# The recurrent block in token products: four convolution tiles computed block by block, the other tiles, states and gate alternating, ScalarE's functions grouped

## The reference

```
def rglru_block(x, w_in, conv_w, conv_b, w_rgate, b_rgate, w_igate, b_igate, lam, w_o):
    gate, u = jnp.split(x @ w_in, 2, axis=-1)
    u = causal_depthwise_conv(u, conv_w, conv_b)          # four taps
    ub = u.reshape(bsz, s, LRU_BLOCKS, LRU_BLOCK_W)
    r = sigmoid(einsum('bshi,hij->bshj', ub, w_rgate) + b_rgate)
    i = sigmoid(einsum('bshi,hij->bshj', ub, w_igate) + b_igate)
    log_a = -LRU_C * r * softplus(-lam)
    a = exp(log_a)
    b_in = sqrt(-expm1(2.0 * log_a)) * (i * u)
    h[t] = a[t] * h[t-1] + b_in[t]                        # the scan
    y = h * gelu(gate)
    return y @ w_o
```

## Time and profile before

| | |
|---|---|
| Median of 3 runs | 2240.7 us (2238.72 to 2241.26) |
| Profiled execution | 2240.25 us |
| Its span in the trace | 2239.0 us |
| Mean granted TensorE clock | 0.974 |
| TensorE busy | 2085.5 us |
| VectorE busy | 1544.3 us |
| ScalarE busy | 1179.8 us |

### The profile page before, as it was taken

The page is one execution under the profiler, slowest core; times in us unless marked ns, Lnnn a source line. Parts: engine busy times, 40 slices in busy tenths (PEclk is TensorE's granted clock), DMA queues, the critical chain, the costliest instruction groups (busy, mean ns, idle before and its releaser), DMA issues.

```text
span 2239.0 us, 33115 instructions
## 1 busy us (share of the span) xinstructions
PE 2085.5 (93%) x13325; PEld 1876.8 (84%) x13325; DVE 1544.3 (69%) x2678; ACT 1179.8 (53%) x2047; POOL 73.5 (3%) x126
## 2 busy tenths in 40 slices
PE   7999999898999989999998998998987999999998
PEld 7778899787799978889987777997976999877997
DVE  4685777787677686576777767777466766666766
ACT  4454555494455555445545536554454555565554
POOL 3000000010000010000000000001000000000000
PEclk9999999999999999999999999999998999999999
DMA  8424566455366654456543436664524666424663
GB/s 262 151 76 142 181 186 186 134 162 183 119 188 181 185 152 129 135 166 192 181 155 130 145 127 190 187 191 133 157 72 148 187 193 183 160 85 148 183 193 107
DMA packets 412008, 356.17 MB, mean 159 GB/s; under 512 B 16242, under 2 KB 353398, under 8 KB 411856
## 3 DMA queue, kind: packets, MB, share of 16 engines
q1 hardware_dynamic: 405104, 332.49, 49.0%
q0 software_dynamic: 6752, 21.57, 2.9%
HBM read 352.97 MB, written 1.05 MB: 158 GB/s over the span
## 4 chain that ended last, share of the span: by engine, by line
PE 79%; DVE 14%; ACT 4%; DMA 2%; issue 1%; POOL 1%; SPq 0%; DVEq 0%; ACTq 0%
PE psum L720 18%; PE psum L722 18%; PE psum L721 18%; PE psum L1230 15%; DVE w_lo L1820 4%; PE psum L1125 3%; PE psum L1111 1%; DVE small L2176 1%; DVE n_tok L2173 1%; PE psum L814 1%; PE psum L895 1%; PE psum L1054 1%; DMA tok<-in_mem_dram 1%; DVE qt L2247 1%; DVE x_tok L2195 1%
## 5 line engine op out<-in xcount | busy, mean ns | idle before, releaser
L1820 DVE TENSOR_TENSOR w_lo<-w_raw,w_hi 128x1024 fp32r<-128x1024 f32 x639 | 749.5, 1220 | 150.3 <-ACT w_hi L1385 149.6
L720 PE MATMUL psum<-xt_hi,w_hi 128*128 128x256 f32 x2424 | 696.1, 287 | 29.4 <-DVE qt L2247 18.4
L721 PE MATMUL psum<-xt_lo,w_hi 128*128 128x256 f32 x2424 | 693.6, 286 | 0.0
L722 PE MATMUL psum<-xt_hi,w_lo 128*128 128x256 f32 x2424 | 693.3, 286 | 0.0
L1385 ACT CAST w_hi<-w_raw 128x1024 fp32r<-128x1024 f32 x639 | 635.5, 1047 | 70.1 <-DMA w_raw<-in_x_w_q_dram 12.7
L720 PEld LDWEIGHTS psum<-xt_hi,w_hi 128*128 128x128 f32 x2424 | 472.3, 195 | 37.5 <-DVE qt L2247 20.1
L721 PEld LDWEIGHTS psum<-xt_lo,w_hi 128*128 128x128 f32 x2424 | 472.3, 195 | 4.8
L722 PEld LDWEIGHTS psum<-xt_hi,w_lo 128*128 128x128 f32 x2424 | 472.3, 195 | 0.0
L720 PE MATMUL psum<-w_hi,xt_hi 128*128 128x512 f32 (+4 forms) x860 | 328.8, 382 | 24.1 <-DVE xt_lo L1835 17.2
L2247 DVE SCALAR_TENSOR_TENSOR qt<-psum,par,qt 128x255 f32<-128x255 f32 (+1 forms) x528 | 218.1, 476 | 170.0 <-ACT qt L1713 170.0
L722 PE MATMUL psum<-w_hi,xt_lo 128*128 128x512 f32 (+4 forms) x860 | 318.4, 370 | 0.0
(11 more groups left out here) (223 smaller groups left out, 1890.7 us busy)
## 6 DMA issues: line engine op xcount, KB each, us to landing
w_raw<-in_f_w_up_dram SPq DMA_DIRECT2D x160, 512.0 KB, 5.4
w_raw<-in_f_w_down_dram SPq DMA_DIRECT2D x88, 512.0 KB, 3.6
w_raw<-in_w_up_dram SPq DMA_DIRECT2D x80, 512.0 KB, 5.3
w_raw<-in_w_down_dram SPq DMA_DIRECT2D x44, 512.0 KB, 3.6
w_raw<-in_x_w_q_dram SPq DMA_DIRECT2D x32, 512.0 KB, 4.6
w_raw<-in_x_w_o_dram SPq DMA_DIRECT2D x32, 512.0 KB, 4.5
w_raw<-in_a_w_qkv_dram SPq DMA_DIRECT2D x24, 512.0 KB, 4.5
w_raw<-in_w_in_fox_dram SPq DMA_DIRECT2D x20, 512.0 KB, 5.0
```

Source lines behind the costliest of these rows:

```text
L720: self.eng.matmul(out, stat[0], mov[0], start=first, stop=False)
L721: self.eng.matmul(out, stat[0], mov[1], start=False, stop=False)
L722: return self.eng.matmul(out, stat[1], mov[0], start=False, stop=last)
L1820: self.up(self.eng.tensor_tensor(self.m.lo[:, s, :], self.m.raw[:, u % RAW, :], self.m.hi[:, s, :].bitcast(F32), ALU.subtract), "w_lo", u)
```

## The change

Three things, in all three engines' `recurrent_block`:

- The first four convolution tiles (features 1024 to 1535 of `b_w_in`) are no longer made by `feature_out` but by `project_blocks`, in tokens by 512 features. ScalarE copies the two results from PSUM to `n_tok` (`keep_first`), and `turned_tile(i)` on TensorE transposes each tile back to features by tokens (two transposes of 128 x 128 a tile). Four weight units serve as before.
- The order: tile 4 stands ahead of the turned tiles, tile 5 behind them; then sigmoid products and single tiles alternate, and two pairs of gate tiles (before: one) stand ahead of the last sigmoid products. Eight tiles have their own list of banks.
- ScalarE's functions are grouped: all sigmoids, both `tanh`, both `exp`, both roots, then GELU. VectorE does both decay pairs one after the other, and the first half's output parts (`lowered(0)`, `lowered(1)`) ahead of the second half's scan.

```diff
+CONV_BANKS = (4, 5, 1, 3, 0, 2, 4, 5)
...
 class Sync:    def recurrent_block(self):
-        for blk in range(KT // 2):
-            self.features(w, D + 2 * blk * P, 2)
-            if blk > 0:
-                self.gate_weights(blk - 1)
-        self.features(w, 0, 2)
-        self.gate_weights(KT // 2 - 1)
-        self.features(w, 2 * P, KT - 2)
+        tile = lambda i, n=1: self.features(w, i * P, n)
+        self.tokens(w, D, BANK)
+        tile(KT + 4)
+        tile(KT + 5)
+        self.gate_weights(0)
+        tile(KT + 6)
+        self.gate_weights(1)
+        tile(KT + 7)
+        tile(0, 2)
+        self.gate_weights(2)
+        tile(2, 2)
+        self.gate_weights(3)
+        tile(4, 4)
...
 class Tensor:    def recurrent_block(self):
+        def turned_tile(i):
+            k = CONV_BANKS[i]
+            self.claim(k)
+            for b in range(TB):
+                self.wait_ge("kept", self.tag, "first", b)
+                ins = self.eng.transpose(m.psum[:, k, b * P:(b + 1) * P], m.n_tok[:, b, i * P:(i + 1) * P], m.ident[:])
+            self.up(ins, "made", self.tag, "u", i)
+            self.free[k] = ("conv", self.tag, i)
...
-        self.turn_now()
-        for blk in range(KT // 2):
-            conv_tiles(blk)
-            if blk > 0:
-                sigmoids(blk - 1)
+        self.project_blocks("first", (6, 7), BANK)
+        conv_tile(4)
+        for i in range(4):
+            turned_tile(i)
+        conv_tile(5)
+        sigmoids(0)
+        conv_tile(6)
+        sigmoids(1)
+        conv_tile(7)
         gate_products(0)
-        sigmoids(KT // 2 - 1)
-        for j in range(1, KT // 2):
-            gate_products(j)
+        sigmoids(2)
+        gate_products(1)
+        sigmoids(3)
+        gate_products(2)
+        gate_products(3)
...
 class Scalar:    def recurrent_block(self):
-        for blk in range(KT // 2):
-            conv_tiles(blk)
-            if blk > 0:
-                sigmoids(blk - 1)
-            self.wait_ge("conv", self.tag, 2 * blk + 1)
-            self.up(self.eng.copy(m.hid[0][:], u[:, 2 * blk:2 * blk + 2, :]), "x_hi", self.tag, blk, 0)
-        decays(0)
-        self.units(2)
-        sigmoids(KT // 2 - 1)
-        decays(1)
-        self.units(2)
...
+        self.keep_first()
+        self.units()
+        for i in (4, 0, 1, 2, 3):
+            base(i)
+        hidden(0)
+        self.units()
+        base(5)
+        sigmoids(0)
+        hidden(1)
+        self.units()
+        base(6)
+        sigmoids(1)
+        hidden(2)
...
+        sigmoids(3)
+        for q in range(2):
+            tanhs(q)
+        for q in range(2):
+            decays(q)
+        self.units(2)
...
 class Vector:    def recurrent_block(self):
+        self.units(KT // 2 + 1)
+        conv(0)
+        conv(1)
+        hidden(0)
+        for i in (4, 2, 3):
+            conv(i)
+        self.units()
+        conv(5)
+        self.units(2)
+        hidden(1)
...
+        self.units(4)
+        decays(0)
+        decays(1)
+        self.units(2)
+        states(0)
+        gated(0)
+        gated(1)
+        self.units(2)
+        lowered(0)
+        lowered(1)
+        states(1)
+        gated(2)
+        lowered(2)
+        gated(3)
+        lowered(3)
```

More of the change, by code:

```diff
@@ L828, in turn_rest @@
         self.x = key
-    def turn_now(self):
-        while self.rest:
-            self.rest.pop(0)()
     def turn_blocks(self, src, tiles, after):
@@ L1520, in sigmoids, with tanhs @@
                 self.up(ins, "kept", self.tag, "sig", blk, q)
-        def decays(q):
+        def tanhs(q):
             h = halves[q]
@@ L1528, in decays @@
             self.up(ins, "act", self.tag, "tanh", q)
+        def decays(q):
+            h = halves[q]
             self.wait_ge("act", self.tag, "tanh", q)
@@ L1537, in gated, with high @@
                     "kept", self.tag, "gate", j)
[L1539 to L1558 removed]
+        def high(j):
             self.wait_ge("prod", self.tag, "gated", j)
@@ L1562, in recurrent_block @@
                     "x_hi", self.tag, "out", 2 * j)
+        self.keep_first()
[12 more added lines that the diff above has]
+        self.units()
+        base(7)
+        self.units(2)
+        sigmoids(2)
+        hidden(3)
+        self.units(2)
[5 more added lines that the diff above has]
+        self.units(2)
+        for q in range(2):
+            self.wait_ge("prod", self.tag, "one_minus", q)
+            self.up(self.eng.activation(th[:, halves[q], :], th[:, halves[q], :], ACT.Sqrt), "act", self.tag, "root", q)
+        gated(0)
+        gated(1)
+        self.units(2)
+        high(0)
+        high(1)
+        gated(2)
+        gated(3)
+        high(2)
+        high(3)
     def rms(self, what, src, width, col):
@@ L1950, in recurrent_block, with conv, hidden, states @@
         self.step(self.eng.tensor_scalar(neg, sp, -LRU_C, None, ALU.mult), self.tag, "lam")
-        def conv_tiles(blk):
-            for i in (2 * blk, 2 * blk + 1):
-                self.units()
-                out = m.psum[:, 4 + i % 2, 0:SEQ]
-                self.wait_ge("base", self.tag, i)
-                for d in range(1, LRU_TAPS):
-                    ins = self.eng.scalar_tensor_tensor(
-                        u[:, i, d:SEQ], out[:, 0:SEQ - d], lru((LRU_TAPS - 1 - d) * KT + i), u[:, i, d:SEQ],
-                        ALU.mult, ALU.add)
-                    if d < LRU_TAPS - 1:
-                        self.after(self.step(ins))
-                self.up(ins, "conv", self.tag, i)
+        def conv(i):
+            out = m.psum[:, CONV_BANKS[i], 0:SEQ]
+            self.wait_ge("base", self.tag, i)
+            for d in range(1, LRU_TAPS):
+                ins = self.eng.scalar_tensor_tensor(
+                    u[:, i, d:SEQ], out[:, 0:SEQ - d], lru((LRU_TAPS - 1 - d) * KT + i), u[:, i, d:SEQ],
+                    ALU.mult, ALU.add)
+                if d < LRU_TAPS - 1:
+                    self.after(self.step(ins))
+            self.up(ins, "conv", self.tag, i)
+        def hidden(blk):
+            self.low(m.hid[1][:], u[:, 2 * blk:2 * blk + 2, :], m.hid[0][:], self.tag, blk, 0, 1)
+            self.call("ready", self.made["ready"], "ready", (self.tag, blk), "hid")
+        def states(q):
+            h = halves[q]
+            self.wait_ge("act", self.tag, "root", q)
+            self.after(self.step(self.eng.tensor_tensor(th[:, h, :], th[:, h, :], ig[:, h, :], ALU.mult)))
+            for j in range(h.start, h.stop):
+                n = self.step(self.eng.tensor_tensor_scan(u[:, j, :], r[:, j, :], th[:, j, :], 0.0,
+                                                          ALU.mult, ALU.add))
+            self.after(n)
         def decays(q):
@@ L1977, in gated, with lowered @@
                     "prod", self.tag, "gated", j)
-        for blk in range(KT // 2):
-            conv_tiles(blk)
-            if blk > 0:
-                self.units(2)
-            self.wait_ge("conv", self.tag, 2 * blk + 1)
-            self.low(m.hid[1][:], u[:, 2 * blk:2 * blk + 2, :], m.hid[0][:], self.tag, blk, 0, 1)
-            self.call("ready", self.made["ready"], "ready", (self.tag, blk), "hid")
-        decays(0)
-        self.units(4)
-        decays(1)
-        self.units(2)
-        for q, h in enumerate(halves):
-            self.wait_ge("act", self.tag, "root", q)
-            self.after(self.step(self.eng.tensor_tensor(th[:, h, :], th[:, h, :], ig[:, h, :], ALU.mult)))
-            for j in range(h.start, h.stop):
-                n = self.step(self.eng.tensor_tensor_scan(u[:, j, :], r[:, j, :], th[:, j, :], 0.0,
-                                                          ALU.mult, ALU.add))
-            self.after(n)
-            if q == 0:
-                gated(0)
-                gated(1)
-            self.units(2)
-        for j in range(KT // 2):
-            if j >= 2:
-                gated(j)
+        def lowered(j):
             pair = slice(2 * j, 2 * j + 2)
```

55 lines of the change are left out of this document (31 added, 24 removed).

## The result

| | before | after |
|---|---|---|
| median of 17 runs each | 2241.26 us | 2245.36 us (2242.8 to 2249.86) |
| ratio | | 1.0019, 95% interval 1.0011 to 1.0027 |
| profiled execution, its span | 2240.25, 2239.0 | 2246.09, 2244.8 |
| mean granted clock | 0.974 | 0.972 |

The changed kernel is slower by 4.1 us at the medians, and by 0.19% by the ratio. The forecast was +2.0 us, half of that, with a range 10 us wide that holds the measured time.

The account below looks back on a forecast made before the run. TensorE, 93% busy, bounds the kernel; the chain behind the last sigmoid product releases its output product. That product 7.9 us later, the chain 6.2 shorter: +1.7 or +2.3, taken as +2.0, so 2242.7 us, range 2236.5 to 2246.8.

Parts of the forecast that it names:

- Term 1, the chain: Recurrent block, from the last sigmoid product's end to the output product: 6.2 us shorter, 22.5 against 28.7 us.
- S: End of TensorE's last sigmoid product in the recurrent block: 479.66 before, forecast at 487.5.
- the cover: ScalarE's root and GELU table loads run under VectorE's decay pairs, with 2.2 us left.
- Term 2, the last sigmoid product: Recurrent block on TensorE: the last sigmoid product ends 7.9 us later, at 487.5 against 479.66.
- unit 8's landing: Weight transfer ahead of the first sigmoid products: takes 4.3 us from its issue at 443.4, landing at 447.7.
- first low part: VectorE's first low part of `hid`, ahead of the first sigmoid products: ready at 454.2, TensorE waiting 4.0 us.
- second low part: VectorE's next low part of `hid`, ahead of the second sigmoid products: ready at 463.8, TensorE waiting 1.5 us.
- The sum at the output product: Start of the first product with `b_w_o`: walked as +1.7 or +2.3 us, taken as +2.0.
- Behind 508.35 nothing is edited ..., so the shift goes through: From the output product to the next norm: the output product's shift passes on unchanged, nothing added.
- The head start: Rival: TensorE has neither wait nor low clock up to sigmoid 3, S at 480.0; 2235.5 us; chance 12%.
- The low clock: Rival: clock low again from 463.9 for 5.2 us, S moves by 2.6 us; 2245.7 with slower landing; chance 16%.
- The slower case: Rival of a low clock holding on between sigmoid 1 and sigmoid 3: 2245.7 us; chance 16%.

Follow-up runs that it names:

- e2: Kernel before, with only VectorE's output parts of the first half moved ahead of the second half's scan; 2237.68 us, ratio 0.9991.
- e7: Kernel before, with only ScalarE's grouping (both tanh, then both exp) and VectorE's decay pairs one after the other; 2243.05 us, ratio 1.0012.
- e4: Kernel before, with two idle VectorE products (2.3 us) added ahead of the first low part of the output operand; 2242.75 us, ratio 1.0014.
- e5: Changed kernel, with two of the four late output weight pieces split before the second half's scan; 2246.15 us, ratio 1.0016.
- e6: Changed kernel, with two of VectorE's four query weight splits in the norm moved behind the first low part of the normed output; 2246.45 us, ratio 1.0023.
- e3: Changed kernel, with the second pair of gate tiles moved behind the last sigmoid products; 2241.59 us, ratio 1.0012.
- e9: e2 plus one of VectorE's four weight parts in the norm moved behind the second low part of the normed output; 2234.96 us, ratio 0.9974.

## Why the prediction was right, and where its size was off

- **Term 1, the chain.** Forecast S + 22.5; measured 22.46 and 22.45 (before 28.7). ScalarE's `tanh` began at S + 1.0 and the first half's `exp` was through at S + 7.3 (7.5 forecast). The loads for root and GELU stayed under cover, but the cover was smaller than walked: the root started at S + 12.1 and takes 1.0 us for a half, which the walk left out, and VectorE wanted it at S + 14.4, so 1.3 us were left and not 2.2. No drain stands beside the table load: 492.98 + 1.28 = 494.26, and `exp` starts at 494.27. By the page "ScalarE: Activation LUTs" of the Trainium skill, section "What ACT_TABLE_LOAD costs", there would be one; neither kernel's rows have it. Of the 6.2 us the order of VectorE's parts alone gave 4.9 (e2), the grouping alone none (e7), and 1.3 came only with all of the change together, some 1.0 of it by ScalarE's earlier cast of `xt_hi`, which the walk did not name.
- **Term 2, the last sigmoid product.** Forecast 7.9 us later, measured 8.5 and 6.9. (The forecast's list of parts, 5.8 and 10.0 less 8.2, adds up to 7.6; its walk gives the 7.9.) By its steps, with 0.47 us taken off: token products end 443.4 (442.2 forecast; the first 18 took 0.35 us each behind the transposes' wait, against 0.30 in the stage I had read them from; in the second execution, at the higher clock, they end at 442.1 on this scale), unit 8's landing 3.9 (4.3), first low part 455.1 (454.2), wait 3.75 (4.0), 24 products in 5.5 (5.2), second low part 464.8 (463.8), wait 1.19 (1.5), then 23.3 us without a gap (23.6). By the fit in "DMA: Bandwidth & Descriptors" of the Trainium skill, section "Anatomy of one DMA", which the page gives for transfers that GpSimd issues, 512 KB would take 3.2 us, as an estimate; this one, issued by SyncE, took 3.9.
- **The sum at the output product.** Forecast +2.0; measured +2.3 and +0.7. The mechanism is the one forecast; that the first execution came within 0.3 us is partly luck, since the clock at the head of the block alone makes 1.2 us between two executions.
- **The step that failed in size: "Behind 508.35 nothing is edited ..., so the shift goes through".** The term was 0 and measured 2.8 and 1.8 us. I had put the second half's scan "behind the first low part, where TensorE is occupied", and looked at TensorE only. VectorE had 4.28 us to spare ahead of the norm, and the scan (3.73 us) took them. The weight parts of `b_w_o` end 6.0 us later from the first transposes (2.3 of it the shift), the four query transfers that wait for them are issued as much later, and the norm's splits wait for the casts. e4 shows that a plain delay does not do this, e5 and e6 that moving the splits takes this wait away.
- **The rivals.** The head start was not kept: the first low part came at 455, not before 451. The low clock did not hold on between sigmoid 1 and 3 (1.00 over 19 us), but it can come back there: in e3 it did, behind a second wait of 2.48 us. The forecast also took the low clock behind the wait of 2.33 us for settled, and in the second execution of the kernel before the clock there was 1.00 over 4.2 us. The slower case's time came out nearly, but by another mechanism.
- **The rest.** In the mean of two executions each, the block up to the norm's transposes (T) is 3.05 us longer: 1.5 at the output product, 1.6 behind it. The spans differ by 5.0 us, since the stages ahead of the block took 2.0 us more in the changed kernel, with the same instructions (425.8 and 427.7 us to the first transposes), and those behind T the same, 1707.5 us both. The medians differ by 4.1 us in both comparisons; the ratios make 4.3 and 3.1. So about 3 us are the change's and explained; whether the 1 us left is the clock's chance ahead of the block (below) or the change's is open.

## What to carry to other kernels

Work taken off one engine's chain goes somewhere: before you count the gain, read that engine's idle time up to the next place where another engine waits for it, here 4.28 us for 3.73 us of scan, and follow the transfers that its later instructions release. A wait filled on TensorE gains nothing where another engine's fixed order stands right behind it, here VectorE's low part or ScalarE's casts that wait for their transfers. Profile both kernels twice before explaining a difference of 2 us.

## What the runs showed of the hardware

The low clock behind a wait is not the same from one execution to the next: behind the norm's wait in the changed kernel it was 0.56 and 1.00, behind the wait of 2.33 us in the kernel before 0.60 and 1.00. At another place it went mostly with the kernel. In `mix0`, far from the change, TensorE waits 2.35 us, ending at 94.0 to 95.5, in every execution. The window behind it, in the kernel before and in the changed one:

```profile
95.00:115.40 20.40, 17.33 (x86) 14.12 (x86) 16.21 (x57) 9.03 (x30) 0.00 (x0) 0.97 0.33 104
```

```profile
95.00:115.40 20.40, 17.42 (x78) 14.41 (x78) 14.14 (x45) 8.60 (x24) 0.00 (x0) 0.92 0.31 105
```

The next wait (3.07 us) ends 18.9 us behind the first in the kernel before, both times, and in e2 and e9; it ends 20.5 us behind it in e4 and e7 and in all eight executions of the changed kernel and of those built on it. The instructions here are the same in all. What decides it I could not find; these 1.6 us, if they are the kernel's own, are most of the 2.0 us by which the stages ahead of the block differ. And a VectorE low part of `hid` took 2.80 us instead of 0.69 where a GpSimd product of 2.71 us ran beside it:

```profile
470.16 2.80 DVE L1878 TENSOR_TENSOR hid_lo<-kt,hid_hi 128x512 fp32r<-128x512 f32 x1
```

```profile
469.70 2.71 POOL L2490 TENSOR_TENSOR e<-e,kt 128x1024 f32<-128x1024 f32 x1 [32.16 <-ACT e L1539]
```
